# Hybrid DeltaNet block on one core: state products of the outputs ahead of the new values, and ScalarE's first mixing splits one step earlier

## The reference, cut to what matters

```
def step(state, inp):
    u_n, w_n, a_n, qd_n, kd_n, gl_n = inp
    v_new = u_n - w_n @ state
    o     = qd_n @ state + a_n @ v_new
    state = state * exp(gl_n) + kd_n.T @ v_new
    return state, o
...
y = sc_b * causal_depthwise_conv(sc_c * sc_h, conv_sc_w)      # short convolution, normed per group
return concatenate([o_gdn, y]) @ w_out                        # "mixing": 8 groups of 128 rows
```

## Time and profile before

| | |
|---|---|
| median of 3 executions | 3179.47 us (3178.14 to 3184.6) |
| profiled execution, its own time | 3183.41 us |
| its span, first to last instruction | 3181.7 us |
| granted TensorE clock, mean over the span | 0.98 of full |
| busy share: TensorE matmuls, weight loads | 95%, 78% |
| busy share: VectorE, ScalarE, GpSimd | 50%, 34%, 40% |
| chain that ended last | TensorE 86%, GpSimd 4%, issue 3%, VectorE 3%, ScalarE 2%, DMA 1% |

### The profile page before, as it was taken

One profiled execution on the slowest core, in us unless ns is written; L12 is line 12 of the kernel. 1 busy time (PEld: TensorE's weight loads), 2 busy tenths in 40 slices (PEclk: granted clock), 3 DMA queues, 4 the chain that ended last, 5 costly groups with the idle time before them and its releaser, 6 DMA issues.

```text
span 3181.7 us, 42915 instructions
## 1 busy us (share of the span) xinstructions
PE 3012.3 (95%) x14494; PEld 2493.3 (78%) x14494; DVE 1591.6 (50%) x2186; ACT 1080.6 (34%) x1992; POOL 1266.4 (40%) x1126
## 2 busy tenths in 40 slices
PE   7899899989998999999989989998999899999998
PEld 6777688868886888888867867886888688888887
DVE  1454455546347444544455545554634744554445
ACT  4532354424133333321133234542323433333112
POOL 6322344434114445444422225443321354545343
PEclk9899999999998999999989999999999999999999
DMA  6523222132021222252232322223112122224321
GB/s 228 183 86 99 83 67 78 54 139 83 32 78 59 87 79 79 79 198 94 98 126 73 102 83 68 75 66 136 57 57 76 53 80 79 79 90 142 144 97 68
DMA packets 131604, 297.13 MB, mean 93 GB/s; under 512 B 11761, under 2 KB 52785, under 8 KB 131505
## 3 DMA queue, kind: packets, MB, share of 16 engines
q1 hardware_dynamic: 69008, 226.07, 21.0%
q10 hardware_dynamic: 62496, 69.78, 6.4%
HBM read 222.37 MB, written 73.43 MB: 93 GB/s over the span
## 4 chain that ended last, share of the span: by engine, by line
PE 86%; POOL 4%; issue 3%; DVE 3%; ACT 2%; DMA 1%; ACTq 0%; SPq 0%; DVEq 0%; POOLq 0%
PE PS L2424 20%; PE PS L2426 20%; PE PS L2425 20%; PE PS L1663 2%; PE PS L1662 2%; PE PS L1661 2%; PE PS L2459 2%; PE PS L1690 2%; PE PS L1694 2%; PE PS L1692 2%; PE PS L2461 2%; PE PS L2463 2%; PE PS L1572 1%; POOL sq_lo L504 1%; POOL am L538 1%
## 5 line engine op out<-in xcount | busy, mean ns | idle before, releaser
L2270 DVE TENSOR_TENSOR h<-h,PS 128x1024 f32<-128x1024 f32 x272 | 331.8, 1221 | 377.7 <-PE PS L2426 240.8
L2424 PE MATMUL PS<-act_hi,w_hi 128*128 128x512 f32 (+1 forms) x1088 | 429.6, 395 | 11.3 <-ACT stage L613 5.8
L1476 DVE TENSOR_TENSOR copied<-copied,PS 128x512 f32<-128x512 f32 x308 | 207.5, 686 | 402.2 <-PE PS L2426 389.4
L2426 PE MATMUL PS<-act_hi,w_lo 128*128 128x512 f32 (+1 forms) x1088 | 407.8, 375 | 0.0
L2425 PE MATMUL PS<-act_lo,w_hi 128*128 128x512 f32 (+1 forms) x1088 | 406.8, 374 | 0.0
L1946 POOL TENSOR_TENSOR w_lo<-raw,w_hi 128x256 fp32r<-128x256 f32 (+1 forms) x144 | 200.7, 1417 | 436.1 <-ACT w_hi L2031 436.1
L562 POOL TENSOR_TENSOR part_lo<-sum_s,part_hi 128x512 fp32r<-128x512 f32 x176 | 232.6, 1323 | 223.3 <-ACT part_hi L1004 223.3
L2424 PE MATMUL PS<-down_hi,mid_hi 128*128 128x512 f32 x704 | 274.1, 389 | 2.7 <-DVE h L2270 2.7
L2424 PE MATMUL PS<-op_t_hi,part_hi 128*128 128x512 f32 x704 | 275.5, 391 | 1.1 <-issue 1.1
L2425 PE MATMUL PS<-op_t_lo,part_hi 128*128 128x512 f32 x704 | 275.3, 391 | 0.0
L2426 PE MATMUL PS<-op_t_hi,part_lo 128*128 128x512 f32 x704 | 275.3, 391 | 0.0
(11 more groups left out here) (321 smaller groups left out, 6220.7 us busy)
## 6 DMA issues: line engine op xcount, KB each, us to landing
raw<-in_w_units SPq DMA_DIRECT2D x156, 512.0 KB, 4.0
gu_raw<-in_w_units SPq DMA_DIRECT2D x64, 512.0 KB, 4.5
a_d<-copied SPq DMA_DIRECT2D x88, 256.0 KB, 2.2
mid_raw<-a_d SPq DMA_DIRECT2D x44, 512.0 KB, 6.6
h<-in_x SPq DMA_DIRECT2D x16, 1024.0 KB, 8.6
qkvz_d<-stage ACTq DMA_DIRECT2D x64, 256.0 KB, 2.5
raw<-att_d SPq DMA_DIRECT2D x32, 512.0 KB, 3.3
prep_raw<-in_w_units SPq DMA_DIRECT2D x16, 512.0 KB, 4.7
```

What stands on the lines that cost most here:

```text
L1476: dve.tensor_tensor(buf[dst][:, :], buf[a][:, :], bank(k), ALU.add)\
L2270: dve.tensor_tensor(h[:, t, :], h[:, t, :], flat(bank(b + 2 * (t % 2), 2)), ALU.add)\
L2424: nc.tensor.matmul(out_ap, whi, xhi, start=start, stop=False)
L2426: return nc.tensor.matmul(out_ap, wlo, xhi, start=False, stop=stop)
```

## The change

Two things are changed. In step o, TensorE makes the four state products first, behind the wait for `qdec_ready` alone, and waits for `vnew_ready` only then; since all four heads' sums are now open in bank 4 at once, only the first product has the start flag and only the last the stop flag. On ScalarE, the two copies of the first mixing rows and the load of the third group's rows, with their two waits, move from the head of `end_act` to step w of the last chunk, right behind the copy to `wt` and ahead of the wait for `vn_full` and the copy to `vnew`.

```diff
@@ chunk_act, step "w"
                     act.activation(hflat(wt[:, :, :]), bank(7), ACT.Copy).then_inc(S["wt_ready"], 1)
                     if not last:
                         exp_decays(act, n + 1, 1 - par)
+                    else:
+                        act.wait_ge(S["sc_full1"], (R + 1) * 3)
+                        mix_hi(act, half, 0)
+                        act.wait_ge(S["y_stored"], (half * 8 + 6) * 16)
+                        load_third(act, half)
@@ end_act
             R = half * 4 + 3
 
-            act.wait_ge(S["sc_full1"], (R + 1) * 3)
-            mix_hi(act, half, 0)
-            act.wait_ge(S["y_stored"], (half * 8 + 6) * 16)
-            load_third(act, half)
             rms_estimate(act, half * TT + TT - 1)
@@ chunk_step_pe, step "o"
-                pe.wait_ge(S["vnew_ready"], n + 1)
                 pe.wait_ge(S["qdec_ready"], n + 1)
                 for hh in range(NH):
                     nc.tensor.matmul(r4(bank(4))[:, hh, :], ge[:, par, hh, :], state[:, hh, :],
-                                     start=True, stop=False)
+                                     start=hh == 0, stop=False)
+                pe.wait_ge(S["vnew_ready"], n + 1)
+                for hh in range(NH):
                     t = nc.tensor.matmul(r4(bank(4))[:, hh, :], dec[par][:, 1, hh, :],
-                                         vnew[:, hh, :], start=False, stop=True)
+                                         vnew[:, hh, :], start=False, stop=hh == NH - 1)
```

## The result

The changed kernel took 3164.80 us (median of 4 executions, 3163.68 to 3167.79), the kernel before, run beside it, 3182.03 us (3178.14 to 3188.01). The ratio is 0.9948, 95% interval [0.9935, 0.996]: 0.5% faster, 17 us by the medians. The forecast was 3156.3 in a range of 3151 to 3169, so the time lies in the range, but the gain is three quarters of the 23.2 us of the sum. The profiled execution took 3163.68 us against 3183.41, and its span is 19.8 us shorter. It is the fastest of the changed kernel's four; the other three, up to 4.1 us slower, have no profile. In the changed kernel the lines from L862 on have moved by a few: the copy to vnew is L867, the state products L1625, the products with vnew L1629, the update L1634, the transposes of v L1556, the small tensor_scalar L1352, the state's update L1358, pass 0's matmuls L2461 to L2465.

What follows compares the result with a forecast made beforehand. TensorE, busy 95% of the span, was taken as the bound, so only closing its holes pays. 10.2 + 0.5 + 5.6 + 6.9 = 23.2 us off a 3179.5 us median gave 3156.3 us, range 3151 to 3169.

Steps and rivals of the forecast that it cites:

- Change 1, middle chunks: TensorE's state products fill the wait for vnew: 0.85 us in each of 12 chunks, 10.2 us, bounds 0.69 and 0.95 each.
- A: Rival: the clock still falls in the shorter hole ahead of pass 0; transitions give 4.0 us each, 3160.8 us; chance 0.18.
- B: Rival: middle chunks give nothing back, TensorE waiting instead for GpSimd's or VectorE's part of the solve; 3166.5 us; chance 0.09.
- C: Rival: the transition's gain is absorbed ahead of pass 1 by loads taking their own time; about 3167 to 3169 us; chance 0.09.
- Change 1, first chunks: At each half's first chunk, a hole of 0.16 us and 0.10 of restart go: 0.25 us each, 0.5 for both.
- Change 2, the copies: ScalarE's two copies, 1.99 us, fit its 2.16 us idle time ahead of vnew; vnew delayed by 0, bounds 0 and 0.45.
- Change 2, pass 0: Pass 0 then waits for VectorE's y product, not GpSimd, and starts at 662.1 instead of 666.13: 4.0 us earlier.
- The clock: With 1.5 us of idle ahead of pass 0 the clock stays at 2.4 GHz: 1.6 and 2.9 us more in the halves.
- Pass 1: Pass 1 moves by the whole 5.6 and 6.9 us; the 4.3 us idle ahead of it stays; cost 0, bounds 0 and 1.
- D: Rival: no change that can be measured, two other rivals together, gain under 6.4 us; 3173 to 3180 us; chance 0.06.
- E: Rival: slower, as ScalarE stands at the moved waits in front of the copy to vnew; 3186 us or more; chance 0.03.

Runs made afterwards that it cites:

- e3: The changed kernel with VectorE's small tensor_scalar of the outputs' sum put behind its four state updates: 3158.55 us, ratio 0.9928 against the kernel before.
- e4: The changed kernel with GpSimd's third product of the decays made to wait until the chunk's state is updated: 3162.64 us, ratio 0.9942 against the kernel before.
- e9: The changed kernel with ScalarE's two copies, the load and their waits behind the last chunk's copy to vnew: 3171.83 us, ratio 0.9967 against the kernel before.
- e8: The kernel before with 18 products nobody needs on TensorE in the hole ahead of pass 0: 3177.61 us, ratio 0.9987.
- e6: The changed kernel with SyncE's two weight loads for pass 1 ahead of the loads of h: 3152.72 us, ratio 0.9908 against the kernel before.
- e5: The changed kernel with 16 products nobody needs on TensorE in the hole ahead of pass 1: 3161.57 us, ratio 0.994 against the kernel before.
- e1: The kernel before with only ScalarE's copies and the load moved, step o left as it was: 3172.05 us, ratio 0.9971.
- e7: The changed kernel with the edits of e3 and e6 together: 3144.73 us, ratio 0.9884 against the kernel before.
- e11: The same kernel as e7, run again: 3146.71 us, ratio 0.9888 against the kernel before.

## Why the prediction was right or wrong

**Change 1, middle chunks: the mis-sized term.** Ten of the 23.2 us were 12 × 0.85. Measured are 0.9 to 1.0 behind the six odd chunks and 0.2 behind the six even ones: about 7.0. The step that failed is the sentence that nothing would be late next, because GpSimd follows TensorE's signals. GpSimd's masks hang on work that lies ahead of vnew: in odd chunks on ScalarE's decays, in even ones on GpSimd's own weight subtractions, which put them 1.9 us later. Moving the outputs by 0.9 us against them slid a 0.17 us operation under a 1.27 us one, and the state's update stands behind it on VectorE. It was to be seen ahead of the change. The earlier trace rows show an odd chunk, where the mask product was over long before the small operation, as these two rows of the kernel before show, and a sum of squares on TensorE gives the state's update more time as well. No even chunk was read.

```profile
513.45 1.27 POOL L519 TENSOR_TENSOR dec<-dec,upto 128x512 f32<-128x512 f32 x1
...
516.51 0.17 DVE L1351 TENSOR_SCALAR ost_t<-ost_ss 128x4 f32<-128x4 f32 x1
```

e3 gives the 0.62 us back, e4 shows the partner. That the weight subtractions make the difference between even and odd is read from the traces, in all middle chunks; no run moved them.

The measured 0.2 lies outside the term's own bounds of 0.69 to 0.95. So the time is in the range because room was left in it for A, B and C, up to 3169, and not because the sum held: by the traces the gain was 19.8 for 23.2, and nearly all that is missing is this term. Of the 8.5 us between 3156.3 and 3164.8, these are 3.4; 2.5 come from the kernel before, whose median is now 3182.0 where 3179.5 was taken, and 2.6 are the difference between the profiled executions (19.8) and the medians (17.2), which no trace explains.

Where nothing interferes, the term was a little small: no restart of 0.32 was seen, and the saving is 0.90, nearer the upper bound of 0.95.

**Change 1, first chunks.** 0.25 each was said, 0.10 and 0.28 measured. In the other runs with this change the first period of half 0 is 36.24 to 36.41, so 0.11 to 0.28.

**Change 2, the copies.** As said, without a delay of vnew.

**Change 2, pass 0.** Start 5.4 us behind vnew, where 657.02 + 5.1 was said: 3.67 us gained, not 4.0. Half of the difference lies behind the y product, which ends at 657.97: pass 0 starts 0.26 us later, where 0.06 was allowed. The other half is the tensor_scalar, which took 0.36 us here, up to the end of GpSimd's subtraction at 656.33. This is what the prediction had put beside the sum from the Trainium skill (SBUF — State Buffer, "Who interferes with whom"), there with 0.3 a half and as not shown by any row; this trace agrees, with 0.19 longer than alone, and in e9 with 1.89. The rule was applied to one place only. Applied to every moved VectorE operation, it would have pointed at the even chunks.

**The clock.** 1.5 and 2.8 us, as e8 has them, where 1.6 and 2.9 were taken. The transitions together gave 5.3 and 7.2 for 5.6 and 6.9. In half 1, 6.3 of the 7.2 are there at pass 1's start, and 0.9 come in pass 1, where the low clock cost more in the kernel before (24.40 us to pass 2 against 23.49).

**Pass 1.** All of the shift arrived, within 0.15 us, and the hole stayed at 4.2 us. e6 confirms the chain over SyncE's order.

**The rivals.** B came true for half of the chunks, at another place than it named. A did not happen in the changed kernel's profile, but it is real, and the changed kernel's other three executions may hold it: of eight halves in four profiles with a hole of 1.88 us (the changed kernel, e4, e5, e6) three fell to the low clock early in pass 0, at 1.6 us each. Of eight with 1.55 to 1.69 us (e1, e3, e7, e11) none did. C, D and E did not come.

## What to carry to other kernels

When an operation is moved earlier on one engine, list what it will run beside there, not only what waits for it: a small VectorE operation that reads SBUF only can cost a whole GpSimd instruction, and all that is queued behind it. Measure its distance to the other engine's work from a common event, here the copy to vnew. Put what others wait for (here the state's update) ahead of such an operation. And read one instance of each kind of iteration, as the slack at the same line can differ between odd and even ones.

## What the runs showed that was not expected

A tensor_scalar on 128x4 elements, from SBUF to SBUF, is held until a running GpSimd product ends: 1.05, 2.06, 0.45 and 0.36 us against 0.17, each time to the end of that product within 0.04 us. A tensor_reduce of 128x512 from SBUF kept its 0.69 us beside the same products, and the state's four updates, with one input in PSUM, their 1.11.

The idle bracket of TensorE understates what a wait costs: 0.46 in the bracket, 0.62 from start to start.

Behind a hole of 1.88 us, with steps ahead of it that have holes themselves, the clock fell in three halves of eight, with the same matmuls at this place in all of them. With 1.55 to 1.69 us of hole there was no such case; eight halves are too few to call that a limit.
